# Second layer's core: heads turned to token-major and the gate projection woven between them

## What is computed

```
proj = u @ w_in                    # q,k (after conv and silu), v, o_pre, i_pre, f_pre
s    = einsum(q, k) * w_intra      # w_intra = exp(d - m_t), causal
num  = einsum(s, v);  den = sum(s) # (the chunked recurrence; the kernel forms it as one 512 x 512 causal product)
h    = num / max(|den|, exp(-m_t))
h    = rms_norm(h, head_g)         # per head
out  = (sigmoid(o_pre) * h) @ w_o
```

## Time and profile before

| | |
|---|---|
| median of 3 runs | 1282.46 us (1279.59 to 1284.38) |
| the profiled execution's own time | 1280.36 us |
| its span, first to last instruction | 1278.6 us |
| mean granted clock of PE | 0.985 |
| busy in the span: PE, PEld | 1220.6, 1009.0 us |
| DVE, ACT, POOL | 665.7, 456.3, 268.5 us |

### The profile page before, as it was taken

One profiled execution on the slowest core, in us unless ns is written; L12 is line 12 of the kernel. 1 busy time (PEld: TensorE's weight loads), 2 busy tenths in 40 slices (PEclk: granted clock), 3 DMA queues, 4 the chain that ended last, 5 costly groups with the idle time before them and its releaser, 6 DMA issues.

```text
span 1278.6 us, 15796 instructions
## 1 busy us (share of the span) xinstructions
PE 1220.6 (95%) x5822; PEld 1009.0 (79%) x5822; DVE 665.7 (52%) x957; ACT 456.3 (36%) x727; POOL 268.5 (21%) x245
## 2 busy tenths in 40 slices
PE   7989999899999999999999998889999999999996
PEld 6767777778888888888888986667888888888885
DVE  6778888544434334344467544985453443443432
ACT  5346666433212212123342235653231221221242
POOL 2312232232102102012201134552120120110221
PEclk9989999899999999999999998989999999999998
DMA  5210101133233232322224221012323223232211
GB/s 183 46 27 23 27 23 49 66 99 99 99 99 99 99 98 98 99 87 89 91 67 132 91 91 50 25 42 66 99 99 99 91 90 112 72 108 92 94 67 66
DMA packets 113887, 104.00 MB, mean 81 GB/s; under 512 B 20934, under 2 KB 112164, under 8 KB 113836
## 3 DMA queue, kind: packets, MB, share of 16 engines
q1 hardware_dynamic: 113804, 103.29, 25.4%
q10 hardware_dynamic: 32, 0.01, 0.0%
HBM read 101.17 MB, written 2.11 MB: 81 GB/s over the span
## 4 chain that ended last, share of the span: by engine, by line
PE 79%; DVE 8%; issue 6%; ACT 3%; POOL 2%; DMA 1%; DVEq 0%; ACTq 0%; POOLq 0%; SPq 0%
PE ps L1479 24%; PE ps L1481 24%; PE ps L1480 24%; DVE nmax L1122 2%; POOL xl L583 1%; DVE xl L981 1%; DVE qtmp L1114 1%; ACT prob L725 1%; ACT uh L739 1%; DVE rinv L1127 1%; ACT whi L640 1%; DMA x_tok<-in_x 1%; DVE diag L1395 1%; ACT xh L711 1%; PE ps L1534 0%
## 5 line engine op out<-in xcount | busy, mean ns | idle before, releaser
L976 DVE TENSOR_TENSOR wlo<-raw,whi 128x2048 fp32r<-128x2048 f32 (+3 forms) x89 | 194.5, 2189 | 157.8 <-ACT whi L640 157.8
L1479 PE MATMUL ps<-xl,whi 128*128 128x512 f32 (+1 forms) x688 | 270.1, 393 | 0.2 <-issue 0.2
L640 ACT CAST whi<-raw 128x2048 fp32r<-128x2048 f32 (+4 forms) x150 | 184.8, 1260 | 239.3 <-PE ps L1481 234.8
L1480 PE MATMUL ps<-xh,whi 128*128 128x512 f32 (+1 forms) x688 | 267.8, 389 | 0.0
L1481 PE MATMUL ps<-xh,wlo 128*128 128x512 f32 (+1 forms) x688 | 267.8, 389 | 0.0
L1479 PE MATMUL ps<-ul,whi 128*128 128x512 f32 x608 | 237.2, 390 | 1.2 <-POOL wlo L531 1.2
L1481 PE MATMUL ps<-uh,wlo 128*128 128x512 f32 x608 | 236.6, 389 | 0.0
L1480 PE MATMUL ps<-uh,whi 128*128 128x512 f32 x608 | 236.5, 389 | 0.0
L561 POOL TENSOR_TENSOR ul<-sq,uh 128x512 fp32r<-128x512 f32 x64 | 83.6, 1307 | 521.3 <-ACT uh L828 521.3
L1204 DVE TENSOR_TENSOR h<-ps,h 128x512 f32<-128x512 f32 x80 | 55.0, 690 | 197.1 <-PE ps L1481 192.5
L1479 PEld LDWEIGHTS ps<-xl,whi 128*128 128x128 f32 (+1 forms) x688 | 128.6, 187 | 28.9 <-issue 2.1
(11 more groups left out here) (242 smaller groups left out, 1628.5 us busy)
## 6 DMA issues: line engine op xcount, KB each, us to landing
raw<-in_mlp_w SPq DMA_DIRECT2D x64, 1024.0 KB, 5.1
raw<-in_mlstm_w_in SPq DMA_DIRECT2D x12, 1024.0 KB, 5.2
raw<-in_mla_w_o SPq DMA_DIRECT2D x4, 1024.0 KB, 4.7
raw<-in_mlstm_w_o SPq DMA_DIRECT2D x4, 1024.0 KB, 4.9
raw<-in_mla_w_in SPq DMA_DIRECT2D x3, 1024.0 KB, 5.7
raw<-in_mla_w_uq SPq DMA_DIRECT2D x16, 192.0 KB, 2.4
x_tok<-in_x SPq DMA_DIRECT2D x4, 512.0 KB, 8.1
mb<-m_rows SPq DMA_DIRECT2D x8, 256.0 KB, 3.2
```

The lines of the kernel that those rows point to most:

```text
L640: last = sc.copy(hi, src)
L976: last = v.tensor_tensor(lo, src, hi.bitcast(F32), ALU.subtract)
L1479: mm(o, ah, bl, start=first, stop=False)
L1480: mm(o, ah, bh, start=False, stop=False)
```

## The change

- The gate projection is token-major: a tile (`gate_tile`) is two halves of 128 tokens x 256 features, 24 matmuls of 256 columns each. Tile 0 comes first, tile 1 between the blocks of head 0's scores, and tile u + 2 in the step of head u, its first half ahead of the numerator and its second inside it. Two PSUM banks (`B_O`) take the tiles in turn. ACT evacuates two tiles (one strip) at a time with the sigmoid straight from PSUM (`gates_out`), once in every second head step. The strips' `split` stands at the end of every second head step.
- The numerator is token-major: for each block of 128 tokens, 128 x 130 or 128 x 128 matmuls with the score parts as weights and the values streaming, 30 a head in place of 12. A column of ones beside the values gives the denominator. `row_sums`, `row_copy`, `head_sums`, `head_diag` and `norm_spread` are gone, and so is `gain`.
- `head_norm` sums the squares with a DVE reduction; `gated` is four DVE operations of 128 x 128 that take the norm factor as a scalar; PE then turns the head with four transposes (`turn_head`) back into the numerator's banks, and `gated_high` and `gated_low` read it there and multiply the gain in.
- The key half is read in place by `st_product`, so `k_copy` is gone. The maxima come by DMA in four pieces a head, POOL masks the diagonal pieces in place (`masked`, four selects), and each block has one exponential.
- The heads are written out instead of looped, and the loads on SP are interleaved anew.

```diff
 (SP)
+            load_max(0)
+            load_max(1)
             for j in range(4):
-                load(N_O + j, cols(w_in, 2 * D + 256 * j))
...
+                load_out(j)
+            for u in range(2, MH):
+                load_max(u)
+                if u % 2:
+                    load_out(3 + u // 2)
...
 (POOL)
+            def head_step(u):
+                if u + 1 < MH:
+                    part_low(u + 1, 0)
+                    part_low(u + 1, 1)
+                if u >= 1:
+                    head_pow(u - 1)
+                if 2 <= u + 2 < MH:
+                    masked(u + 2)
+                if u + 1 < MH:
+                    part_low(u + 1, 2)
+                    part_low(u + 1, 3)
...
 (ACT)
-                last = sc.activation(wt[:, z % 2, 0:P], md[:, e, P * j:P * j + P], ACT.Exp, bias=bias, scale=-1.0)
-                if j < TT - 1:
-                    last = sc.activation(wt[:, z % 2, P:LEN[j]], mb[:, e, P * (j + 1):S], ACT.Exp,
-                                         bias=bias, scale=-1.0)
+                sc.activation(wt[:, z % 2, 0:LEN[j]], mx[:, e, TRI[j]:TRI[j] + LEN[j]], ACT.Exp,
+                              bias=gcol[:, MH * j + u:MH * j + u + 1], scale=-1.0).then_inc(w_exp, 1)
...
+            def gates_out(j):
+                for i in range(2):
+                    act.wait_ge(gemm_done, T_O + 2 * j + i + 1)
+                    for half in range(2):
+                        tt = 2 * i + half
+                        last = sc.activation(sg[:, tt, 256 * (j % 2):256 * (j % 2) + 256],
+                                             ps[:, B_O[i], 256 * half:256 * half + 256],
+                                             ACT.Sigmoid, scale=rcol[:, tt:tt + 1])
+                    last.then_inc(gemm_evac, 1)
+            def head_step(u):
+                if u >= 1:
+                    square_num(u - 1)
+                if u + 1 < MH:
+                    high(u + 1, 0)
+                    weights(u + 1, 2)
+                    high(u + 1, 1)
+                if u >= 0 and u % 2 == 0:
+                    if u >= 4:
+                        act.wait_ge(hs_ready, u - 2)
+                    gates_out(u // 2)
+                if u >= 2:
+                    gated_high(u - 2)
+                if u + 1 < MH:
+                    v_high(u + 1)
+                    weights(u + 1, 3)
+                    high(u + 1, 2)
+                    if u + 2 < MH:
+                        weights(u + 2, 0)
+                    high(u + 1, 3)
+                    if u + 2 < MH:
+                        weights(u + 2, 1)
+                if u >= 0 and u % 2:
+                    split(N_O + 2 + u // 2)
...
 (DVE)
+            def gated(u):
+                e, j = u % 2, u // 2
+                dve.wait_ge(gemm_evac, T_O + 2 * j + 2)
+                dve.wait_ge(rc2_ready, u + 1)
...
+                last.then_inc(hs_ready, 1)
+            def head_step(u):
+                if u + 1 < MH:
+                    weighted(u + 1, 0)
+                    weighted(u + 1, 1)
+                if u >= 1:
+                    head_norm(u - 1)
+                if u >= 2:
+                    gated_low(u - 2)
+                if u + 1 < MH:
+                    weighted(u + 1, 2)
+                    v_low(u + 1)
+                    weighted(u + 1, 3)
+                if u >= 0 and u % 2:
+                    split(N_O + 2 + u // 2)
+                if u >= 1:
+                    gated(u - 1)
...
 (PE)
+            def gate_tile(t, halves=(0, 1)):
+                j, i = t // 2, t % 2
+                s = (N_O + j) % 2
+                if 0 in halves:
+                    strip_ready(N_O + j)
+                    pe.wait_ge(gemm_evac, T_O + t - 1)
...
+            def turn_head(u):
+                pe.wait_ge(hs_ready, u + 1)
+                for t in range(TT):
+                    last = tr(num(u)[:, t, 0:P], hs[u % 2][:, P * t:P * t + P], ident[:])
+                last.then_inc(hs_turn, 1)
...
+            def head_step(u):
+                if u + 1 < MH:
+                    st_product(u + 1, 0)
+                    st_product(u + 1, 1)
+                if u >= 2:
+                    turn_head(u - 2)
+                if u < 6:
+                    gate_tile(u + 2, (0,))
+                elif u == 7:
+                    out_products2(range(2, 4))
+                numerator(u, (0, 1, 2))
+                if u + 1 < MH:
+                    st_product(u + 1, 2)
+                if u < 6:
+                    gate_tile(u + 2, (1,))
+                elif u == 6:
+                    out_products2(range(0, 2))
+                numerator(u, (3,))
+                if u + 1 < MH:
+                    st_product(u + 1, 3)
...
+            out_products2(range(4, 5))
+            turn_head(MH - 2)
+            out_products2(range(5, 6))
+            turn_head(MH - 1)
+            out_products2(range(6, 8))
```

More of the change, by code:

```diff
@@ L135, in trunk @@
         r_b = sb("r_b", [P, S])
+        diag_at = (nc.sbuf_base + 31) // 32 * 32
         diag = sb("diag", [P, 2, S])
@@ L599, in _ @@
[L599 to L614, removed]
@@ L889, in high @@
[L889 to L902, removed]
-                sc.activation(numsq[:, e, :], bank(B_NUM[e]), ACT.Square).then_inc(num_sq, 1)
@@ L937, in _ @@
-            for j in range(4):
-                split(N_O + j + 1)
-                if j == 3:
-                    for block in range(TT):
-                        weights(0, 0, block)
-                for m in (2 * j, 2 * j + 1):
-                    if m == 7:
-                        act.wait_ge(gemm_done, T_O + 8)
-                        high(0, 0, 0)
-                        high(0, 0, 1)
-                        v_high(0, 0)
-                    act.wait_ge(gemm_evac, T_O + m + 1)
-                    sc.activation(sg[:, m, :], otmp[:, m % 2, :], ACT.Sigmoid).then_inc(sig_new, 1)
@@ new lines, in high, with v_high, square_num @@
+            def high(u, j):
+                z = 4 * u + j
+                act.wait_ge(sw_mul, z + 1)
+                sc.copy(swh(u % 2, j), sw[z % 2][:, 0:LEN[j]]).then_inc(sw_hi, 1)
+            def v_high(u):
+                sc.copy(mvh[:, u % 2, :, 0:P], v_tok[:, :, P * u:P * u + P]).then_inc(mv_hi, 1)
+            def square_num(u):
+                if u >= 2:
+                    act.wait_ge(hs_turn, u - 1)
+                act.wait_ge(num_mm, u + 1)
+                sc.activation(blocks(hs[u % 2][:, :]), num(u)[:, :, 0:P], ACT.Square).then_inc(num_sq, 1)
@@ L962, in _ @@
+            split(N_O + 1)
+            act.wait_ge(acc_add, adds_before(NORM_MLP1))
+            act.wait_ge(stat_col, NORM_MIX1 + 1)
+            act.wait_ge(gemm_evac, T_O)
+            weights(0, 0)
+            weights(0, 1)
+            for u in range(-1, MH):
+                head_step(u)
+            square_num(MH - 1)
+            gated_high(MH - 2)
+            gated_high(MH - 1)
             residual_stage(N_WO2, T_WO2, NORM_MLP1, G_MLP + 8)
@@ L1437, in _ @@
-            v_low(0, 0)
-            weighted(0, 0, 2)
-            weighted(0, 0, 3)
-            for u in range(3):
-                if u == 2:
-                    dve.wait_ge(sg_ready, MH)
-                head_step(0, u, first=(u == 0), early=(u < 2))
-            with dve.Fori(1, MPAIRS - 1) as i:
-                own.enter(i, 1, 6)
-                head_step(i, 1)
-                head_step(i, 2)
-                own.leave(1, MPAIRS - 1)
-            head_step(MPAIRS - 1, 1, last=True)
-            gated(MPAIRS - 1, 0)
@@ L1456, in _ @@
+            split(N_O + 1)
+            for u in range(-1, MH):
+                head_step(u)
+            head_norm(MH - 1)
+            gated(MH - 1)
+            gated_low(MH - 2)
+            gated_low(MH - 1)
             dve.wait_ge(wlo_ready, N_WO2 + 2)
```

428 lines of the change are left out of this document (140 added, 288 removed).

## The result

The changed kernel takes 1297.03 us (median of 4 runs, 1296.66 to 1298.78) against 1283.42 us (1279.59 to 1285.53) for the kernel before in runs taken with it; the ratio is 1.0112, 95% interval [1.0085, 1.0139]. So it is slower, by about 14 us, where 1285 with a range up to 1296 was forecast. The kernel before spreads by itself: beside the first four experiments its 22 executions lay between 1276.87 and 1285.66 us, so a difference of 2 or 3 us between medians says little. One of the ten executions of experiment 1 took 6847.87 us, at a granted clock of 1.00, and is not in its ratio. The span of the profiled execution grew from 1278.6 to 1295.0 us, the mean granted clock fell from 0.985 to 0.973.

The account below looks back on a forecast made before the run. PE was taken to bound the whole kernel, DVE the heads. The stretch's 136.8 against 140.7 us saved 3.9, clock spells added 6.3, net +2.4: 1282.46 + 2.4 = 1284.9, rounded 1285; range 1265 to 1296.

Parts of the forecast that it names:

- The path through the even steps: Steps 2 and 4: after T (PE finishes a head's scores), split chain holds PE until T + 10.4; 20.15 us.
- The clock: Heads: idle time in steps 2, 4 and 6 brings lower clock, 2.1 us each, 6.3 us more.
- Rival 3: Heads: waits in steps 0, 2, 4 and 6 each bring 6.4 us at half clock; 1291 us, chance 0.20.
- Score blocks "should change nothing, since the columns stay": Heads on PE: only 64 rows holding a key should add no time to the score blocks.
- Odd steps: "no wait for a bank": Odd head steps: PE-bound, transposes without a wait for a bank; 11.35 us a step, step 1 11.0.
- The tail: Step 7 up to the second output strip: low parts of the last two heads set the end, 15.3 us.
- Startup: Stretch before T of step 0: first gate tiles and head 0's score blocks, 13.5 us.
- The sum: Changed stretch, gate projection through heads: 13.5 plus steps 123.3 gives 136.8 us against 140.7; clock adds 6.3.
- rival 2: Heads: split not on the path, steps 2, 4 and 6 shorter, clock stays up; 1263 us, chance 0.20.
- rival 4: Heads: no spells at the lower clock at all; 1278.6 us, chance 0.10.
- rival 5: Even steps on ACT: a table change empties ACT first, 1.28 us counting twice in each of four; 1290 us, chance 0.03.
- The rule on transposes: PE in the heads: transposes do not count as busy for the clock gate; no extra charge.

Follow-up runs that it names:

- experiment 1: split_mid: the changed kernel with the strips' splits moved, on ACT and DVE, to the middle of odd steps; 1282.14 us, ratio 1.0005.
- experiment 2: The changed kernel with the two gate tiles' sigmoids moved on ACT ahead of the last cast of the odd step before; 1285.66 us, ratio 1.0025.
- experiment 5: fill: the changed kernel with the second score block computed eight times more in steps 2, 4 and 6; 1297.19 us, ratio 1.0123.
- experiment 7: k128: the changed kernel with score products reading all 128 rows instead of the head's 64; 1292.21 us, ratio 1.0087.
- experiment 3: The changed kernel with both moves, those of experiment 1 and experiment 2; 1271.39 us, ratio 0.9919.
- experiment 4: The changed kernel with the gate's sigmoid replaced by an exponential, so no table loads between the heads; 1291.50 us, ratio 1.0075.
- experiment 8: experiment 3 with high part moved earlier on ACT, low part on DVE, and step 6's first output products ahead of the numerator; 1257.08 us, ratio 0.9812.
- experiment 6: experiment 2 with block 1 of the next head's scores computed twelve times more in steps 2, 4 and 6; 1283.42 us, ratio 1.0009.

## Why the prediction was wrong, point by point

Two terms of the sum failed. The price of score blocks on 64 rows was put at nothing, and the runs show 3 to 5 us. The lower clock was charged 6.3 us and took about 9.6, because step 0 was left out and step 6 put too low. The rest is small waits that the hand-followed path did not see. The chain itself, which makes up most of the waiting of PE, was right.

- *The path through the even steps:* right. The split's cast and subtraction ahead of the gating, the weighting behind it, the table load, the sigmoids: all in the order and nearly at the sizes given. PE's gate tile starts at T + 11.0 (794.80 - 783.80) where 10.4 was said, in step 0 at T + 5.3 where 4.9 was; the numerator of step 6 at T + 13.0 where 12.65 was. Together 0.4 + 0.6 + 0.6 + 0.3 = 1.9 us. Experiments 1 and 2 show both halves of the chain, one by one.
- *The clock:* right in kind, too small: this step failed in size. Charged were 2.1 us in each of steps 2, 4 and 6. Counted from the matmuls that start 0.21 instead of 0.12 apart, or at twice their distance in other shapes, with the slow first one, the loss is about 2.0 us in step 0, 1.8 in step 2, 2.4 in step 4 and 3.4 in step 6 (numerator, score block and output products): 9.6, which is 3.3 more than charged. The slow transposes (1.11 instead of 0.66) are not in it, since experiment 5 shows that they cost nothing in steps 2 and 4. More than half of the 3.3 is step 0, which I left out though its wait was in my own sum (3.65 us, from 1.25 to 4.9), because a wait of 3.08 had been followed by no spell. One row was weak ground for that, and the same trace spoke against reading the waits by their length: the spells from 826.0 and 858.0 came behind waits of 1.60 and 1.51 us only, while waits of 1.47, 1.49 and 1.58 had none behind them. The first of these:

```profile
826.24 1.12 PE L1886 MATMUL ps<-diag,ones 128*128 128x512 f32 x2 [1.60 <-DVE diag L1395]
```

  Rival 3 charged 3.2 in each of steps 0, 2, 4 and 6, 12.8 in all; 9.6 lies halfway between it and my 6.3.
- *Score blocks "should change nothing, since the columns stay":* this step failed. The kernel before had no product of 64 rows at all ahead of the heads or in them, so no row could give a price, and it was put at nothing without one. A block of 64 rows between products of 128 costs 0.34 us (experiment 7), and the places together 3.9 us in the profiled stretch (4.8 by the medians, 3.2 by the ratios), a whole term of the sum that was zero. In even steps the blocks ahead of the wait cost nothing; in steps 1, 3 and 5 all count.
- *Odd steps: "no wait for a bank":* nearly right. But the numerator waits 0.76 us for the low part of the head two back in steps 3 and 5, and the transposes 0.25 us for DVE: 2.0 us that the hand-followed path, which took DVE to be free there, missed. The wait for the low part, 6.7 us in the changed kernel with the 5.18 of step 6, took 10.1 us in experiment 3, set free of the larger ones.
- *The tail:* 16.6 instead of 15.3. The transposes of heads 5 and 7 wait 1.42 and 1.17 us there.
- *Startup:* 754.90 - 740.77 = 14.1 instead of 13.5, three places with blocks of 64 rows again.
- *The sum:* the stretch was to last 136.8 + 6.3 = 143.1 and lasted 156.1, 13.0 more. The terms: clock 3.3, blocks of 64 rows 3 to 5, path 1.9, the small waits of odd steps 2.0, tail 1.3: 11.5 to 13.5. They overlap a little, and the blocks of 64 rows are the least certain. With the 0.9 us lost ahead of the stretch, which nothing here explains, this is the miss of the profiled execution (1296.78 against 1282.8).
- *Readings:* two of the rows were read too freely. The prediction says of the three gaps that each waits for ACT's or DVE's results; the row of the 2.99 us has `issue`, so the profile shows nothing that it waited for. And 0.227 us a matmul is not the distance shown, 0.23; it is right over many (33 distances from 896.88 to 904.38 give 0.227), and nothing hangs on it.
- *Rivals:* rival 2 (the split not on the path) is ruled out by experiment 1, rival 4 by the clock of the windows, rival 5 by experiment 4. Rival 3 came nearest in sign and time (1291) but knew only the clock, not the terms that were missing. The rule on transposes (the Trainium skill, "TensorE: Matmul & The Clock Gate", section "PE-mode transpose") was not put to the test by an experiment. The one long group, 16 transposes of 3.67 us at 8.02 us in the kernel before, stands behind a wait of 3.49 us at a granted clock of 1.00, and full clock follows it; that does not bear the rule out, but a single case at the start of the program does not refute it.
- *The range:* every term left out here was positive. A path followed has each wait that one sees and none that one doesn't, so the error was likelier on the slow side, and the range, 20 us below the forecast and 11 above, had it the other way round.

## What to carry to other kernels

When long work of two engines in turn (a strip's cast of 1.88 us on ACT, then its subtraction of 2.29 on DVE) is put ahead of small operations that PE waits for, PE pays for both, every time round: experiment 1 gave 13.7 us for three places, 4.6 each. Put it where its engines would wait anyway, as early as its input and its slot allow, and then look again, since the next chain comes out from behind it. Here two moves gave 14 and 11 us, both together 25, and three more small ones another 14 (by the ratios). Where a path is followed, expect small waits at handoffs between engines that the path doesn't show (here 0.25, 0.76, 1.17 and 1.42 us), and let the range lean to the slow side.

## What the runs showed of the hardware

- The lower clock level does not follow from the length of the last wait alone. The 12 waits of 3.2 to 4.0 us ahead of gate tiles (in the changed kernel, fill, split_mid and k128) were each followed by 15 to 23 matmuls at half clock, and so was one of 2.46 us in experiment 4 (23). Waits of 2.37 and 1.70 us in experiment 3 were followed by about 16 and 28, after 2.8 and 1.0 us at full clock. One of 3.08 us in the kernel before was followed by none. The wait of 1.42 us in step 7 was followed by full clock in the changed kernel (transposes 0.66 us) and by half clock in experiment 8 (1.11 us). One spell came where no wait was above 0.76 us (experiment 6). Idle time can bring the level, as experiment 6 shows by filling it; what else counts is open.
- A float32r score block of 64 rows between products of 128 rows takes 0.34 us longer than the same columns on 128 rows: distances of 0.21, 0.22, 0.12, 0.21 and 0.22 us instead of 0.11, 0.17, 0.12, 0.12 and 0.12 (experiment 7, block 2 of step 0). Within the block nothing is lost.
- A table load cost its 1.28 us and hardly more: 1.29 to 1.42 us in four places (experiment 4).
